# Start of the second block: which engine copies which half of x, and the order in which the halves of x are transposed and normalised

## The reference, cut to what matters

```python
x = x + ga2 * hierarchical_moe(h2, ...)          # end of block 1
h = rms_norm_2(x, norm_mix_g_2[layer])           # start of block 2
z = h @ w_in_2[layer]                            # 1024 -> 5640 columns
```

## Time and profile before

| what | before |
|---|---|
| median of 3 runs | 1146.41 us (1145.62 to 1146.78) |
| the profiled execution | 1145.27 us, of which 1143.5 us are its span |
| mean granted TensorE clock | 0.997 |
| PE busy | 1117.0 us (98%) |
| DVE busy | 484.7 us (42%) |
| ACT busy | 415.2 us (36%) |
| POOL busy | 184.6 us (16%) |
| share of PE in the chain that ended last | 90% |

### The profile page before, as it was taken

One profiled execution on the slowest core, in us unless ns is written; L12 is line 12 of the kernel. 1 busy time (PEld: TensorE's weight loads), 2 busy tenths in 40 slices (PEclk: granted clock), 3 DMA queues, 4 the chain that ended last, 5 costly groups with the idle time before them and its releaser, 6 DMA issues.

```text
span 1143.5 us, 15501 instructions
## 1 busy us (share of the span) xinstructions
PE 1117.0 (98%) x5884; PEld 753.6 (66%) x5884; DVE 484.7 (42%) x968; ACT 415.2 (36%) x617; POOL 184.6 (16%) x79
## 2 busy tenths in 40 slices
PE   5899999999999999999999998999999999999998
PEld 3689777874444444444444444978878888888887
DVE  4585343662222222222222214789574653333226
ACT  4544543331111111111111115675465354354334
POOL 0303133000000000000000002200314064433532
PEclk9999999999999999999999999999999999999999
DMA  9968668789999999999999997453424366555532
GB/s 354 371 235 294 201 254 304 286 363 401 422 422 423 422 423 424 423 424 422 424 422 422 422 424 290 148 179 117 148 94 162 126 218 201 167 184 177 191 115 107
DMA packets 96974, 331.75 MB, mean 290 GB/s; under 512 B 8545, under 2 KB 31570, under 8 KB 71314
## 3 DMA queue, kind: packets, MB, share of 16 engines
q1 hardware_dynamic: 96640, 330.58, 74.7%
q0 software_dynamic: 80, 0.26, 0.1%
q10 hardware_dynamic: 194, 0.06, 0.0%
HBM read 329.84 MB, written 1.05 MB: 289 GB/s over the span
## 4 chain that ended last, share of the span: by engine, by line
PE 90%; DMA 3%; DVE 2%; ACT 2%; SPq 2%; issue 1%; DVEq 0%
PE ps L1289 19%; PE ps L908 15%; PE ps L909 15%; PE ps L910 15%; PE ps L1329 9%; DMA ring<-in_w_in 3%; PE ps L1266 3%; PE ps L1267 2%; PE ps L1344 1%; PE ps L995 1%; SPq L775 1%; PE ps L1345 1%; PE ps L1452 1%; DVE ring_r L2137 1%; PE ps L975 1%; ACT ring_r L1669 1%
## 5 line engine op out<-in xcount | busy, mean ns | idle before, releaser
L870 POOL TENSOR_TENSOR ring_r<-ring,ring_r 128x1024 fp32r<-128x1024 f32 x66 | 172.2, 2630 | 832.6 <-ACT ring_r L1669 832.5
L909 PE MATMUL ps<-ring_r,hl_r 128*128 128x512 f32 (+1 forms) x536 | 211.0, 394 | 0.0
L908 PE MATMUL ps<-ring_r,hl_r 128*128 128x512 f32 (+1 forms) x488 | 196.8, 403 | 4.1 <-DVE hr_r L2229 3.9
L910 PE MATMUL ps<-ring_r,hr_r 128*128 128x512 f32 (+1 forms) x488 | 192.0, 393 | 0.0
L1669 ACT ACTIVATE ring_r<-ring 128x2048 fp32r<-128x2048 f32 x88 | 163.7, 1909 | 49.1 <-PE ps L910 35.5
L2137 DVE TENSOR_TENSOR ring_r<-ring,ring_r 128x2048 fp32r<-128x2048 f32 x55 | 129.7, 2368 | 73.9 <-ACT ring_r L1669 73.6
L1289 PE MATMUL ps<-ring,arena 128*64 128x512 f32 x688 | 154.7, 599 | 0.0
L909 PEld LDWEIGHTS ps<-ring_r,hl_r 128*128 128x128 f32 x536 | 101.5, 189 | 21.6
L908 PEld LDWEIGHTS ps<-ring_r,hl_r 128*128 128x128 f32 x488 | 92.2, 189 | 30.0 <-DVE hr_r L2229 5.4
L1289 PEld LDWEIGHTS ps<-ring,arena 128*64 128x64 f32 x688 | 48.9, 138 | 93.0 <-issue 91.6
L910 PEld LDWEIGHTS ps<-ring_r,hr_r 128*128 128x128 f32 x488 | 92.3, 189 | 21.7
(11 more groups left out here) (383 smaller groups left out, 1819.3 us busy)
## 6 DMA issues: line engine op xcount, KB each, us to landing
ring<-in_w SPq DMA_DIRECT2D x64, 2048.0 KB, 22.9
ring<-in_w_in SPq DMA_DIRECT2D x20, 2048.0 KB, 10.9
gates<-in_w SPq DMA_DIRECT2D x22, 1024.0 KB, 22.7
ring<-in_w_ada SPq DMA_DIRECT2D x16, 1024.0 KB, 9.5
arena<-in_w SPq DMA_DIRECT2D x11, 1024.0 KB, 19.5
uy<-in_w SPq DMA_DIRECT2D x11, 1024.0 KB, 21.5
ring<-in_w_ffn_gate SPq DMA_DIRECT2D x11, 1024.0 KB, 5.5
ring<-in_w_ffn_up SPq DMA_DIRECT2D x11, 1024.0 KB, 8.0
```

The lines of the kernel that those rows point to most:

```text
L870: nc.gpsimd.tensor_tensor(rest[:, a:b], w[:, a:b], lead[:, a:b].bitcast(F32), ALU.subtract).then_inc(sem("w_rest_b"), 1)
L908: mm(o, lhsT=a_lead, rhs=b_lead, start=start, stop=False, skip_group_check=True)
L909: mm(o, lhsT=a_lead, rhs=b_rest, start=False, stop=False, skip_group_check=True)
L910: return mm(o, lhsT=a_rest, rhs=b_lead, start=False, stop=stop, skip_group_check=True)
```

## The change

Three edits, all at the start of block 2.

1. The copies swap engines and places. DVE copies the two left halves of x, ahead of its part of the weights of `fq`. ACT copies the two right halves, behind the four leads of the first pair (0,0).
2. The order of the pairs is `XM` = (0,0), (1,0), (0,1), (1,1), both left halves first, in `small_order`, on ACT and on DVE; the counts that PE waits for follow.
3. PE transposes only the two left halves ahead of `fq0`. The two right halves are transposed in the middle of `fq0`, between k = 3 and k = 4, as `middle` of `token_rows`.

```diff
-        small_order += [f"xm{t}{h}" for t, h in TH]
+        XM = [(t, h) for h in range(2) for t in range(TT)]
+        small_order += [f"xm{t}{h}" for t, h in XM]
...
             def hm_ready(t, k):
-                return sem("norm_rest"), KD * t + k + 1
+                return sem("norm_rest"), 4 * XM.index((t, k // 4)) + k % 4 + 1
...
-            for t, h in TH:
-                pe.wait_ge(*x2_ready(t, h))
-                transposes(f"xm{t}{h}", x[:, t, :], h)
+            def x2_transposes(h):
+                for t in range(TT):
+                    pe.wait_ge(*x2_ready(t, h))
+                    transposes(f"xm{t}{h}", x[:, t, :], h)
+
+            x2_transposes(0)
...
-                    token_rows(name, chunk_name, u, hm_ready, middle)
+                    token_rows(name, chunk_name, u, hm_ready, middle if name != "fq0" else lambda: x2_transposes(1))
...
             lead_weights(M["fq"])
+            norm_leads("xm", "norm_mix_g_2", XM[0:1])
             for t in range(TT):
-                act_.wait_ge(sem("moe_combined"), 4 * PAIRS - 3 + t)
-                af(x[:, t, 0:COL], dense.bank(f"moe{2 * t}"), ACT.Copy).then_inc(sem("x2_left"), 1)
-            norm_leads("xm", "norm_mix_g_2", TH)
+                act_.wait_ge(sem("moe_combined"), 4 * PAIRS - 1 + t)
+                af(x[:, t, COL:], dense.bank(f"moe{2 * t + 1}"), ACT.Copy).then_inc(sem("x2_right"), 1)
+            norm_leads("xm", "norm_mix_g_2", XM[1:4])
...
+            for t in range(TT):
+                dve.wait_ge(sem("moe_combined"), 4 * PAIRS - 3 + t)
+                v.tensor_copy(x[:, t, 0:COL], dense.bank(f"moe{2 * t}")).then_inc(sem("x2_left"), 1)
             rest_weights(M["fq"])
-            for t in range(TT):
-                dve.wait_ge(sem("moe_combined"), 4 * PAIRS - 1 + t)
-                v.tensor_copy(x[:, t, COL:], dense.bank(f"moe{2 * t + 1}")).then_inc(sem("x2_right"), 1)
-            for t in range(TT):
-                norm_rests(0, "xm", "norm_mix_g_2", t)
+            for n, (t, h) in enumerate(XM):
+                src = small.ready(dve, f"xm{t}{h}")
+                dve.wait_ge(sem("norm_lead"), 4 * n + 4)
+                for j in range(4):
+                    k = 4 * h + j
+                    v.scalar_tensor_tensor(rest_h[:, k, t * P:(t + 1) * P], src[:, j * P:(j + 1) * P], pc("norm_mix_g_2", k, 1),
+                                           lead_h[:, k, t * P:(t + 1) * P].bitcast(F32), ALU.mult,
+                                           ALU.subtract).then_inc(sem("norm_rest"), 1)
```

More of the change, by code:

```diff
@@ L427, in two_blocks @@
                 small_released[f"mt{tag}{t}{h}"] = sem("merged_rest"), n + 1 + 4 * SECOND[tag]
-            for i, name in enumerate(("xm", "xf", "xp")):
+            small_released[f"xm{t}{h}"] = sem("norm_rest"), 4 * XM.index((t, h)) + 4
+            for i, name in enumerate(("xf", "xp"), 1):
                 small_released[f"{name}{t}{h}"] = sem("norm_rest"), TT * KD * i + 4 * n + 4
@@ L1487, in _ @@
                     at = ATT2_AT.get((name, "mid"))
+                    assert name != "fq0" or at is None
                     middle = None if at is None else lambda: attention_step("_b", att2[at])
-                    token_rows(name, chunk_name, u, hm_ready, middle)
+                    token_rows(name, chunk_name, u, hm_ready, middle if name != "fq0" else lambda: x2_transposes(1))
                 if name == "fq0":
```

## The result

| | before | changed |
|---|---|---|
| median of 22 runs each | 1145.90 us (1144.70 to 1147.74) | 1148.53 us (1145.84 to 1151.12) |
| the profiled execution | 1145.27 us, span 1143.5 | 1146.07 us, span 1144.3 |
| mean granted clock there | 0.997 | 0.999 |

The ratio is 1.0025, with a 95% interval of 1.0018 to 1.0032: slower by 2.6 us between the medians, 2.1 to 3.7 by the interval. The profiled execution of the changed kernel is one of its quickest three. So its trace cannot hold the whole difference, and the runs have to be read beside it. The 22 runs of the changed kernel lie in three clusters: three at 1145.8 to 1146.2 us with mean clocks of 0.998 to 0.999, nine at 1147.5 to 1148.6 with 0.994 to 0.997, ten at 1150.1 to 1151.1 with 0.991 to 0.994.

A forecast was written before the change was run, and what follows sets the result against it. PE, busy in 98% of the span, was taken to bound the kernel. Earlier start -1.32, transposes inside `fq0` +0.79 and wait +1.55 gave +1.02 on 1146.41: 1147.4 us, range 1145.6 to 1149.2.

The forecast's parts named there:

- the forecast's own: Range of the main forecast for the whole kernel's median, 1146.4 to 1148.4 us; that forecast had chance 0.58.
- slower by over 0.2%: Outcome for the whole kernel: slower by more than a measurement can tell from no change, 2.3 us; chance 0.12.
- What lies beside: Work beside `fq0`: squares 1.9 us later, POOL's second half of `hf` at about 722.6, still in time with 0.9 us cover.
- the +1.0 is handed on: Behind `fq1`: all engines wait for PE, so the 1.0 us delay reaches the end; the wait near 768 absorbs nothing.
- the clock rival: Start of block 2: second idle of 1.55 us brings a clock fall costing 1.75, total +2.8 us, 1149.2; chance 0.16.
- the prediction's own sign: Around `fq0`: the prediction is wrong if the clock from 702 to 714 us is not 1.00.
- the late-DVE rival: Behind the experts: a skipped branch stalls DVE past 700.3, so its copies come late; +1.5 us, 1147.9; chance 0.13.

The follow-up runs named there:

- e4: Kernel before with only DVE's and ACT's copies swapped, all transposes ahead of `fq0`: 1146.82 us, ratio 1.0009.
- e9: Changed kernel without the middle transposes, all transposes ahead of `fq0`; copies swapped and new pair order kept: 1147.27 us, ratio 1.0012.
- e6: Changed kernel with the right transposes moved from behind k = 3 to behind k = 1 of `fq0`: 1146.51 us, ratio 1.0007.
- e1: Changed kernel run again with no edit, for a second profile: 1150.75 us over 5 runs, ratio 1.0039.
- e5: Changed kernel with the copies on the engines of before; new pair order and middle transposes kept: 1150.77 us, ratio 1.0042.
- e8: Changed kernel with two matmuls of no use in PE's second idle only, behind the right transposes: 1149.74 us, ratio 1.0033.
- e12: Kernel before with ACT's leads of `hf` ahead of the squares and DVE's rest of `hf` ahead of the row factors: 1147.32 us, ratio 1.0015.
- e2: Changed kernel with matmuls of no use in both PE idles, five in the first, two in the second: 1147.81 us, ratio 1.0019.
- e3: Kernel before with four matmuls of no use in its 2.2 us idle ahead of the first transposes: 1145.98 us, ratio 1.0004.
- e7: Changed kernel with five matmuls of no use in PE's first idle only: 1147.57 us, ratio 1.0014.
- e10: Changed kernel with the right transposes behind k = 1 of `fq0` and four matmuls of no use in the first idle: 1146.03 us, ratio 1.0000.
- e11: Changed kernel, right transposes behind k = 1, first idle filled, `hf` leads ahead of squares, `hf` rest ahead of row factors: 1147.54 us, ratio 1.0015.

## Why the prediction was right, and which size was off

**The frame.** The median, 1148.53, lies in the range (1145.6 to 1149.2), just outside the forecast's own (1146.4 to 1148.4), and on the side that was forecast. The size of the change is off: 2.6 us instead of 1.0. That the absolute time looks closer is luck, since the 1146.41 that it was counted from is a median of three runs and lies 0.5 above that of the 22. And the 0.12 given to "slower by over 0.2%" stood for what the interval now makes the likeliest case.

**Edit 1** was forecast at -1.32 and gave -1.20 of `fq0`. Each step came as written: copies in DVE's old idle, transposes right behind the experts, ACT's leads as soon as the weights were done. The 0.12 that is missing lies in ACT's weights, which end 1.73 us behind the experts instead of 1.59, after a wait for their load; the scatter of `fq0` between profiles is as large. e4 and e9 add that the gain needs the other edits: edit 1 alone starts `fq0` at 4.66, edits 1 and 2 at 4.27.

**Edits 2 and 3**: the transposes were to cost 0.79 and a wait of 1.55 was to follow. The chain from the transposes to k = 4 was 2.29 instead of 2.34, so 0.79 and 1.50; the profile's own figure of 1.25 for the idle counts from a modelled end. The second half of `fq0` took 2.92 instead of 2.81, since its first product follows an idle. Together -1.20 + 2.29 + 0.11 = **+1.20** where I had +1.02. e6 shows the mechanism by itself: with work for PE during the latency, the wait is gone and `fq0` takes 1.41 less.

**What lies beside**: the squares start 2.0 later (forecast 1.9), POOL's second piece of `hf` ended in time, no product of `hf0` waited. But the step "the +1.0 is handed on" was 0.25 short. POOL's piece of `hf` and the copy behind it moved onto DVE's norm of the queries. POOL after, DVE after, and DVE before, in their timelines:

```profile
716.07 5.95 POOL L872 TENSOR_TENSOR ring_r<-ring,ring_r 128x1024 fp32r<-128x1024 f32 x2 [8.03 <-ACT ring_r L1675]
722.09 1.04 POOL L889 COPY arena<-cst 64x1024 f32<-64x1024 f32 x1
```

```profile
721.40 0.66 DVE L2532 SCALAR_TENSOR_TENSOR fz<-fz 128x16 f32<-128x16 f32 x1
721.98 0.16 DVE L2533 TENSOR_SCALAR fz<-fz 128x16 f32<-128x16 f32 x1
722.17 2.03 DVE L2077 TENSOR_TENSOR spp<-arena 128x1024 f32<-128x1024 f32 x1
```

```profile
720.88 1.02 DVE L2520 TENSOR_SCALAR fz<-fz 128x16 f32<-128x16 f32 x1
721.94 1.23 DVE L2070 TENSOR_TENSOR spp<-arena 128x1024 f32<-128x1024 f32 x1
```

From the first `fz` instruction to the end of this norm's first product DVE needs 0.4 us more than before. I had asked of POOL only whether it is late for PE, not whom it meets.

**The step that failed is the clock rival's.** The prediction put it at 1.75 us and 0.16, on the ground that "the idle ahead of block 2 stays as long as it was" and "the idle of 2.2 us in the trace before did not bring it". The size of one fall was nearly right (1.55 in e1). The chance was not: the fall at 705 is in the profiles of e1, e5, e8 and e9. So by the prediction's own sign, a clock of 1.00 from 702 to 714, the first profile bears it out and e1, with 0.66 from 705 to 710, does not. The fall is not in the profiles of before, e12, the changed kernel's first, e4 (2.9 us of idle there) and e6 (2.2), and in none with the first idle filled (e2, e3, e7, e10, e11). Of the 1148.53 - 1145.90 = 2.63 us between the medians, 2.63 - 1.45 = 1.2 are not the structure that the first profiles show. Filling takes 0.7 (e2, both idles) and 1.0 (e7, the first alone) of it back against the same 22 runs. That the rest is falls too is not shown. What I had not looked at is that idle and products changed places. In the kernel before, 2.2 us of idle were followed by sixteen transposes; in the changed one PE has eight, and then idle of 2.5 us. The stretch without products is shorter, 3.4 us instead of 4.6, and yet it is the one behind which the clock falls. That the order is what decides is not shown either: e4 has 2.93 us of idle with twelve transposes behind it and no fall, e9 has 2.49 with eight and a fall, and the changed kernel has one in one profile and none in the other.

**A second fall, near 772,** is in the profiles of e1, e5, e6, e7, e8 and e10, where PE's wait for DVE there is 1.2 to 1.3 us, and in none of before, e3, e4, e9, e11 and e12, where it is 0.94 to 0.96. The changed kernel's first profile and e2 have the wait of 1.2 without the fall. That the 0.2 us of DVE's delay brings it is argued from this, not shown; e11 took the delay away and had no fall, in one profile.

**What stays open:** how many of the 22 runs had which fall (their profiles are not there); how much of each run's time lies ahead of the change, where the profiles differ by up to 2.1 us; and why e4, whose positions are those of before, measured 0.7 us above the median of before beside it. e9 measured 1.3 above, and the fall of its profile would be enough for that if most of its runs have it.

**The two rules of the skill.** "TensorE: Matmul & The Clock Gate", Part 4, of the Trainium skill does not count transposes as work for the clock; by it the longer stretch of the kernel before, 4.6 us, was all idle for the clock. In its profile and in that of e12 the clock stayed at 1.00 there, so these traces do not bear it out. "Runtime: NRT & Kernel Launch", Instruction fetch mechanics, of the Trainium skill lets a taken branch stall the engine. DVE's first copy stood 0.3 us behind its last work of the experts and was released by PE, so here the skipped branch cost it nothing that shows, and the late-DVE rival falls.

## What to carry to other kernels

A chain transpose, lead, rest, product has a latency (2.3 us here) that is paid once per batch; cutting the batch in two pays it twice unless PE has that much independent work between the second transposes and their first use. Place the second batch by that length (k = 1, not k = 3). Where a change moves idle time of PE, count the clock too: here the longer path cost 1.45 us and 1.2 more are left in the median, of which a few matmuls of no use in the idle took back 0.7 to 1.0. And one profile is one execution: that of the changed kernel had no fall, that of e1, the same kernel, had two.

## What the hardware showed that was not expected

A vector instruction on two columns, 0.16 us elsewhere in the same list, took 2.08 us while POOL ran a subtraction of two f32 operands, and one that takes 0.17 took 0.89 beside POOL's copy (e12; in e11 2.06 and 0.89). The POOL rows of e12:

```profile
711.21 5.08 POOL L870 TENSOR_TENSOR ring_r<-ring,ring_r 128x1024 fp32r<-128x1024 f32 x2 [3.15 <-ACT ring_r L1669]
716.35 1.06 POOL L887 COPY arena<-cst 64x1024 f32<-64x1024 f32 x1
```

The two long ones end at 716.30 and 717.43, where POOL's piece and POOL's copy end. Not all of DVE's work is touched: its sixteen rests from 705.03, the first of them beside POOL's piece of `fq`, took 4.23 us, no more for each than the eight of the earlier trace rows, 2.16. So it is short links like those of the row factors that have to be kept away from POOL's pieces here.
